# Gated delta rule: 32x32 diagonal blocks inverted on VectorE beside the gate projection, two TensorE levels left

## What is computed

```
proj = x @ w_in                      # q, k, v (3 x 1024 columns), gate z (1024), a, b
q, k, v = silu(causal_conv4(proj[qkv]))
q = l2_norm(q) * 128**-0.5;  k = l2_norm(k)
beta = sigmoid(b);  g = cumsum(-exp(A_log) * softplus(a + dt_bias))      # per chunk
decay[i, j] = exp(g[i] - g[j]) for i >= j
lower = strictly_lower((k * beta) @ k.T * decay)
u, w = solve(I + lower, [v * beta, k * beta * exp(g)])      # unit lower triangular
attn = (q @ k.T) * decay
for each chunk:                      # S is the 128 x 128 state of a head
    v_new = u - w @ S
    o = (q * exp(g)) @ S + attn @ v_new
    S = S * exp(g_last) + (k * exp(g_last - g)).T @ v_new
o = rms_norm(o) * silu(z);  mix = o @ w_out
```

## Time and profile before

| | us |
|---|---|
| three timed runs | 2270.66, 2274.2, 2274.4 (median 2274.2) |
| the profiled execution, own time | 2272.42 |
| its span in the profile | 2270.7 |
| column loop: first convolution 43.7 to last qkv matmul 175.8 | 132.1 |
| gate steps to the end of block 1 (175.8 to 252.0) | 76.2 |
| delta rule, block 2 (252.0 to 449.2) | 197.2 |
| mixer output, block 3 (449.2 to 523) | 73.8 |
| everything behind it | 1747 |

### The profile page before, as it was taken

The page is one execution under the profiler, slowest core; times in us unless marked ns, Lnnn a source line. Parts: engine busy times, 40 slices in busy tenths (PEclk is TensorE's granted clock), DMA queues, the critical chain, the costliest instruction groups (busy, mean ns, idle before and its releaser), DMA issues. The chain is left out here.

```text
span 2270.7 us, 35278 instructions
## 1 busy us (share of the span) xinstructions
PE 2089.2 (92%) x9789; PEld 1580.8 (70%) x9789; DVE 1512.7 (67%) x2511; ACT 1307.8 (58%) x2174; POOL 478.7 (21%) x367
## 2 busy tenths in 40 slices
PE   7998899899999999999995899999999999999994
PEld 6875799885677677777764655685766766777772
DVE  3762556556788778878773314746877777888884
ACT  3333244533687777877774223532777777777774
POOL 0000355400122222322221300001232222222220
PEclk9999999999999999999998799998999999999997
DMA  5321100015799999999998110026999999999994
GB/s 189 102 82 56 43 20 20 20 44 213 292 371 372 356 351 356 369 365 368 359 351 266 47 60 29 32 76 241 333 346 349 355 354 345 367 366 370 372 361 144
DMA packets 181905, 539.80 MB, mean 238 GB/s; under 512 B 26528, under 2 KB 58176, under 8 KB 181696
## 3 DMA queue, kind: packets, MB, share of 16 engines
q1 hardware_dynamic: 151776, 460.75, 54.2%
q0 software_dynamic: 25248, 69.25, 12.1%
q10 hardware_dynamic: 4800, 8.78, 1.0%
HBM read 504.71 MB, written 54.10 MB: 246 GB/s over the span
## 5 line engine op out<-in xcount | busy, mean ns | idle before, releaser
L1779 DVE TENSOR_TENSOR gu_l<-ring,gu_h 128x1024 fp32r<-128x1024 f32 x512 | 610.2, 1220 | 98.2 <-ACT gu_h L1643 82.0
L1643 ACT CAST gu_h<-ring 128x1024 fp32r<-128x1024 f32 x512 | 523.2, 1059 | 88.2 <-DMA ring<-in_moe_w_up 72.4
L1558 PE MATMUL bank<-gu_h,xgT_l 128*128 128x512 f32 x1024 | 413.5, 404 | 0.0
L1560 PE MATMUL bank<-gu_h,xgT_h 128*128 128x512 f32 x1024 | 401.3, 392 | 0.0
L1559 PE MATMUL bank<-gu_l,xgT_h 128*128 128x512 f32 x1024 | 400.4, 391 | 0.0
L1907 POOL DMA_INDIRECT xg<-h_rows,list_idx x128 | 146.9, 1147 | 904.2 <-issue 476.4
L1610 PE MATMUL bank<-ring,hmT_f 128*128 128x512 f32 x536 | 273.3, 591 | 0.0
L1650 ACT CAST down_h<-ring 128x1024 fp32r<-128x1024 f32 x128 | 134.1, 1047 | 221.2 <-DMA ring<-in_moe_w_down 131.8
L1926 POOL DMA_INDIRECT moe_sum<-y,out_idx x128 | 196.8, 1538 | 171.8 <-issue 152.6
L1785 DVE TENSOR_TENSOR down_l<-ring,down_h 128x1024 fp32r<-128x1024 f32 x128 | 156.7, 1225 | 103.9 <-ACT down_h L1650 96.6
L1560 PEld LDWEIGHTS bank<-gu_h,xgT_h 128*128 128x128 f32 x1024 | 192.9, 188 | 42.4
(11 more groups left out here) (375 smaller groups left out, 3351.8 us busy)
## 6 DMA issues: line engine op xcount, KB each, us to landing
ring<-in_moe_w_gate SPq DMA_DIRECT2D x256, 512.0 KB
ring<-in_moe_w_up SPq DMA_DIRECT2D x256, 512.0 KB
ring<-in_moe_w_down SPq DMA_DIRECT2D x256, 512.0 KB
ring<-in_a_w_in SPq DMA_DIRECT2D x32, 512.0 KB
ring<-in_a_w_out SPq DMA_DIRECT2D x8, 512.0 KB
h_rows<-ring ACTq DMA_DIRECT2D x8, 512.0 KB, 2.6
moe_sum<-y ACTq DMA_DIRECT2D x8, 512.0 KB, 6.3
ring<-moe_sum SPq DMA_DIRECT2D x8, 512.0 KB, 5.0
```

The source lines that it names most:

```text
L1558: nc.tensor.matmul(out, lhsT=xl, rhs=wh, start=k == 0, stop=False)
L1560: last = nc.tensor.matmul(out, lhsT=xh, rhs=wh, start=False, stop=k == KD - 1)
L1643: nc.scalar.copy(gu_h[:, c, :, :], gate_up_cols(gate_slot, c * CH // 2, CH // 2)).then_inc(gu_hi.sem, 1)
L1779: nc.vector.tensor_tensor(gu_l[:, c, :, :], gate_up_cols(gate_slot, c * CH // 2, CH // 2), gu_h[:, c, :, :].bitcast(F32), ALU.subtract).th ...
```

## The change

**What it does.** The decay, the products of keys and queries, and the inverse of all 128 diagonal 32x32 blocks move out of block 2 into block 1. In the column loop PE makes the sums of g behind c = 2, ACT reads them at c = 3 and stores them to DRAM, loads them back to all partitions at c = 4 (2 MB), builds the distances (32 operations of 128x128) at c = 6 to 13 and their exponentials (128x2048) at c = 9 and 13. From c = 17 on PE makes two units of key products per column and DVE multiplies them with the decay. ACT packs the diagonal blocks (strided copies), DVE transposes them so that one partition holds whole systems, and eliminates 31 columns (two operations each) between the gate steps; the inverses are transposed back at the end of block 1. The squares shrink to the 8 columns of q and stand beside gate steps 10 to 13, and ACT instead of DVE takes the gate out of PSUM, through Silu. In block 2 two levels remain (32 to 64: `product5`, `inverse5`; 64 to 128: `product6`, `inverse6`), and those of tile tt + 1 are issued among the scan of tile tt. The constants shrink from 17 planes to 7. Since the system takes ring slots 10 and 11, x is loaded a second time in block 2; w_out is loaded there too, and the router's weights have a tile of their own.

The scan of a tile and the inverse of the next one alternate. The diff, cut to its core:

```diff
+                def gate_rows():
+                    act.wait_ge(cols_ready.sem, cols_ready.base + 1)
+                    nc.scalar.activation(ecol[:, :, :, :], bank[3][:, 0:2 * TT * H].rearrange("p (a t h) -> p a t h", a=2, t=TT), ACT.Exp)
+                    nc.scalar.activation(gcol_neg[:, :, :], bank[3][:, 0:TT * H].rearrange("p (t h) -> p t h", t=TT), ACT.Copy, scale=-1.0)
+                    nc.scalar.copy(row_parts, bank[2][0:H, :].rearrange("p (t q) -> p t q", q=P))
+                    link(act, "act", nc.scalar.activation(row_parts2, bank[2][0:H, :].rearrange("p (t q) -> p t q", q=P), ACT.Exp))
+                    for kind, rows in enumerate((row_parts, row_parts2)):
+                        act.dma_start(gain_row[kind].rearrange("t h q -> h t q"), rows).then_inc(row_stored.sem, 16)
+                def load_gate_rows():
+                    act.wait_ge(row_stored.sem, row_stored.base + 32)
+                    act.dma_start(sym, gain_row[0].partition_broadcast(P)).then_inc(gate_rows_in.sem, 16)
+                def distances(first):
+                    if first == 0:
+                        act.wait_ge(gate_rows_in.sem, gate_rows_in.base + 16)
+                    tt, h0 = divmod(first, H)
+                    for h in range(h0, h0 + 4):
+                        last = nc.scalar.activation(sym[:, tt, h, :], sym[:, tt, h, :], ACT.Abs, bias=gcol_neg[:, tt, h:h + 1])
+                    if first % 16 == 12:
+                        link(act, "act", last)
+                def decays(half):
+                    nc.scalar.activation(sym[:, 2 * half:2 * half + 2, :, :], sym[:, 2 * half:2 * half + 2, :, :], ACT.Exp, scale=-1.0).then_inc(sym_done.sem, 1)
+                def pack(half):
+                    act.wait_ge(kq_done.sem, kq_done.base + 2 * KQ_PAIRS * (half + 1))
+                    for b in range(QUADS):
+                        dst = packed[quad(b), :, 2 * H * half:2 * H * (half + 1)]
+                        src = ring[quad(b), 10 + half, :].rearrange("p (m q) -> p q m", q=P)[:, quad(b), :]
+                        last = nc.scalar.copy(dst, src)
+                    last.then_inc(packed_done.sem, 1)
...
+                    if c == 3:
+                        gate_rows()
+                    elif c == 4:
+                        load_gate_rows()
+                    elif 6 <= c < 14:
+                        distances(4 * (c - 6))
+                        if c in (9, 13):
+                            decays((c - 9) // 4)
+                    elif c == N_QKV - 2:
+                        pack(0)
+                act_z_hi(act, 0)
+                act_z_hi(act, 1)
+                pack(1)
+                for n in range(2, 2 * KD):
+                    if n >= KD + 4:
+                        square_pair(n - KD - 4)
                     act_z_hi(act, n)
+                    if n == KD - 2:
+                        act.wait_ge(norms_ready.sem, norms_ready.base + 1)
+                        nc.scalar.activation(k_norm[:, :, :], k_norm[:, :, :], ACT.Sqrt).then_inc(k_root.sem, 1)
+                    elif n == KD + 1:
+                        act_open_gate(act, 0)
...
+                    if c == 2:
+                        gate_sums()
                     if c > 2 * H:
                         transpose_v(c - 1 - 2 * H)
+                        keys_queries(2 * (c - 1 - 2 * H))
+                        keys_queries(2 * (c - 1 - 2 * H) + 1)
+                for u in range(2 * H - 2, KQ_UNITS):
+                    keys_queries(u)
...
+                    if KD + 2 <= n < KD + 6:
+                        sum_squares(2 * (n - KD - 2))
+                        sum_squares(2 * (n - KD - 2) + 1)
+                    elif n == KD + 6:
                         transpose_sums()
...
+                def decayed(u):
+                    tt, pair = divmod(u, KQ_PAIRS)
+                    if u % (2 * KQ_PAIRS) == 0:
+                        v.wait_ge(sym_done.sem, sym_done.base + u // (2 * KQ_PAIRS) + 1)
+                    v.wait_ge(kq_ready.sem, kq_ready.base + u + 1)
+                    c0 = tt % 2 * H * P + pair * 2 * P
+                    dst = ring[:, 4 + tt // 2:11 + tt // 2:6, c0:c0 + 2 * P].rearrange("p a (h q) -> p a h q", q=P)
+                    src = kq_bank(u)[:, :].rearrange("p (h a q) -> p a h q", a=2, q=P)
+                    by = sym[:, tt, 2 * pair:2 * pair + 2, :].unsqueeze(1).to_broadcast([P, 2, 2, P])
+                    nc.vector.tensor_tensor(dst, src, by, ALU.mult).then_inc(kq_done.sem, 1)
...
+                def systems():
+                    v.wait_ge(packed_done.sem, packed_done.base + 2)
+                    own(nc.vector.transpose(ring[:, 9, 0:BLOCK], ring[:, 8, 0:BLOCK]))
+                    own(nc.vector.tensor_single_scalar(sq_sys[:, :], ring[:, 9, 0:BLOCK:SUB + 1], EPS, ALU.add))
+                    nc.vector.transpose(k_norm[:, :, :].rearrange("p t h -> p (t h)"), sq_sys[:, :]).then_inc(norms_ready.sem, 1)
+                    own(nc.vector.reciprocal(gain_sys[:, :], sq_sys[:, :]))
+                    own(nc.vector.tensor_tensor(gain_sys[:, :], gain_sys[:, :], beta_sys[:, :], ALU.mult))
+                    own(nc.vector.tensor_tensor(lower, lower, gain_sys[:, :].unsqueeze(2).to_broadcast([P, SUB, SUB]), ALU.mult))
+                def eliminate(j):
+                    rows, cols = SUB - 1 - j, j + 1
+                    part = outer[:, 0:rows * cols].rearrange("p (i c) -> p i c", c=cols)
+                    own(nc.vector.tensor_tensor(part, lower[:, j + 1:, j:j + 1].to_broadcast([P, rows, cols]), solved[:, j:j + 1, 0:cols].to_broadcast([P, rows, cols]), ALU.mult))
+                    own(nc.vector.tensor_tensor(solved[:, j + 1:, 0:cols], solved[:, j + 1:, 0:cols], part, ALU.subtract))
+                def inverses():
+                    by = gain_sys[:, :].unsqueeze(1).to_broadcast([P, SUB, SUB])
+                    own(nc.vector.tensor_tensor(X_sys.rearrange("p (c i) -> p i c", i=SUB), solved, by, ALU.mult))
+                    own(nc.vector.tensor_tensor(Y_sys.rearrange("p (i c) -> p i c", c=SUB), solved, by, ALU.mult))
+                    nc.vector.transpose(ring[:, 8, BLOCK:2 * BLOCK], X_sys)
+                    nc.vector.transpose(ring[:, 9, BLOCK:2 * BLOCK], Y_sys)
...
+                    if c > 2 * H:
+                        decayed(2 * (c - 1 - 2 * H))
+                        decayed(2 * (c - 1 - 2 * H) + 1)
+                dve_z_lo(v, 0)
+                for u in range(2 * H - 2, KQ_UNITS):
+                    decayed(u)
+                dve_z_lo(v, 1)
+                v.wait_ge(z_identity.sem, z_identity.base + 2)
+                systems()
+                low, spent = 2, 1.8
+                for j in range(SUB - 1):
+                    while low < KD + 6 and spent >= 1.8:
+                        dve_z_lo(v, low)
+                        low, spent = low + 1, spent - 1.8
+                    eliminate(j)
+                    spent += 0.4 + 0.00208 * (SUB - 1 - j) * (j + 1)
+                for n in range(low, KD + 6):
                     dve_z_lo(v, n)
+                copy_sums()
+                dve_z_lo(v, KD + 6)
+                dve_z_lo(v, KD + 7)
+                inverses()
+                norms()
...
+                for tt in range(-1, TT):
+                    ahead = tt + 1 < TT
+                    for g in range(2):
+                        if tt < 0:
+                            keys_T(0, g)
+                        elif tt > 0:
+                            from_state(tt, g)
+                        if ahead:
+                            product5(tt + 1, g)
+                    for g in range(2):
+                        if tt >= 0:
+                            from_values(tt, g)
+                        if ahead:
+                            inverse5(tt + 1, g)
+                    for g in range(2) if ahead else ():
+                        if tt >= 0:
+                            keys_T(tt + 1, g)
+                        transpose_X(tt + 1, g)
+                        product6(tt + 1, g)
+                    for g in range(2) if ahead else ():
+                        inverse6(tt + 1, g)
+                    for g in range(2) if ahead else ():
+                        values_keys(tt + 1, g)
...
+                def systems_x(tt):
+                    act.wait_ge(x_done.sem, x_done.base + 2 * tt)
+                    for b in range(QUADS):
+                        nc.scalar.copy(X0[quad(b), :, quad(b)], X_packed[quad(b), :, H * tt:H * tt + H].rearrange("p c h -> p h c"))
+                    for b in (0, 2):
...
+                systems_y(0)
+                act_open_gate(act, 1)
+                for tt in range(-1, TT):
+                    ahead = tt + 1 < TT
+                    if tt >= 1:
+                        root(tt - 1)
+                    for g in range(2) if ahead else ():
+                        act.wait_ge(p5_ready.sem, p5_ready.base + at(tt + 1, g))
```

(35 more changed lines are left out.)

837 lines of the change are left out of this document (309 added, 528 removed).

## The result

| | before | after |
|---|---|---|
| median of 4 runs, us | 2272.43 | 2194.94 |
| lowest, highest | 2268.09, 2274.4 | 2189.83, 2197.87 |
| profiled execution, own time | 2272.42 | 2189.83 |

The ratio of after to before is 0.9659, 95% interval 0.9647 to 0.9671: 77.5 us less. The forecast was 2182 with a range of 2158 to 2214. The changed kernel, run again later beside other kernels, gave 0.9657 (0.9638 to 0.9676).

The account below looks back on a forecast made before the run. TensorE was taken to bound block 2, and a ring as full as TensorE the column loop. −2 + 35.7 − 14.2 − 111.2 = −91.7 from 2272.4 gives 2180.7, stated as 2182 us; range 2158 to 2214.

Parts of the forecast that it names:

- full ring: Column loop: convolution, Silu, rounding and low part wait on each other, 5.51 us per column; ScalarE work behind the Silu adds.
- rival A: Column loop absorbs ScalarE's distances and exponentials in slack, so 25 us go: 2157 us; chance 12%.
- the exponentials: Column loop: two of 128x2048 at 1.95 us, each with two table loads of 1.28 and links: 4.6 each, 9.2 together.
- c = 3 and 4: Column loop: an exponential and a Silu with table loads, four small activations, three DMA issues; 5.2 us including sums of g.
- Rival D: ScalarE: a table switch costs as much again as its load, 6 × 1.28, 8 us: 2190 us; chance 5%.
- The sums of squares: Gate steps 10 to 13 carry them on TensorE, 0.86 us each; these steps take 14.3 us.
- Rival B: Gate steps: VectorE bounds them through elimination and low parts, packs and inverses at doubled price; 14 more, 2196 us; chance 18%.
- The packs: Before gate step 2: ScalarE packs four strided blocks of 32x512, 0.6 to 1.05 us each.
- the hand-overs: Block 2: copies and subtractions passing between engines from product5 to inverse6 lie beside the state's products in the scan.
- the prologue: Start of block 2, tile 0's inverse with nothing beside it: VectorE places blocks for 4.5 us; 19 us in all.
- rival C: Block 2: TensorE's clock stays at 1.2 GHz through the prologue and one scan tile, about 20 us more: 2202; chance 12%.
- Rival E: Pauses at c = 3, 4, 9 and 13 lower TensorE's clock lastingly: +96, +38 and +70, about 2390 us; chance 3%.

Follow-up runs that it names:

- the added operations: Against the changed kernel, the first of the two operations of each eliminated column is issued twice, 31 more on VectorE: ratio 0.9676 (0.9661 to 0.9690).

## Why the prediction held, and which terms were off

**Column loop, +35.7 against +33.1.** The reading as a full ring was right, and rival A (work absorbed) is refuted by the run without distances: 16.4 us came back for the work taken out. Distances cost 6.69 − 5.51 = 1.18 per column (forecast 1.2), the sums of g 1.3 (1.3), key products 1.8 per column (1.73). The term that was too large is the exponentials: 3.2 us each for two of them where 4.6 was taken, since the second load lies beside the convolution. The same held at c = 3 and 4: 3.6 and 0.4 us in place of 5.2. What the forecast had at nothing is the clock inside the loop: 1.3 us in column 14. Rival D, a switch dearer than its load, is refuted: it was cheaper, and in the rows the exponential starts 1.30 us after the load (105.27 and 106.57), so nothing is added between the load and a long activation, which the rows of before had left open.

**Gate steps, −14.2 against −10.3.** Step 2 starts 15.5 us after the last column's matmuls, as forecast. Two terms were missed. The sums of squares take 1.8 us a step, not 0.86; the forecast counted one column of squares per step where there are two. And a pause of 3.75 us ahead of step 2 lowers the clock to 0.66 for 5 us. Rival B, VectorE as the bound, is refuted by the added operations: there were about 8 us of room. The packs cost 1.1 us each, just above the upper end.

**Block 2, −111.2 against −98.6.** The work on TensorE was right: once the wait is gone an iteration takes 19.8 us (forecast 19.6 to 20.8). What failed is the sentence that the hand-overs lie beside the state's products: the copies of u and w stand ahead of them, and nothing is beside these. ScalarE's placing was priced (4 to 6 us; it is 6.6), but put ahead of u and w in the prologue alone, and there with 3 of it seen (the wait was 3.87). It stands in the same place in the iterations of tiles 0 and 1 too, and holds up the whole scan. Moving half of it gave back 12 us. The second miss is the prologue: VectorE's clearing and placing 8.8 us, not 4.5; handing X to ScalarE gave 3.7. From the block's start to the first scan 25.5 us go by where the forecast had 19.

**The clock (rival C)** was right in part, and in addition to the forecast rather than in place of it: the waits cost a second time, 1.6 us an iteration by the run with products in the waits, where the forecast had 2.5 us for all of block 2. The measured 2194.9 is near the 2196 of rival B, but by another mechanism, so that is chance. Rival E didn't come near: the column loop ran at 0.96. (Its own terms add to 204 us, so the 92 us that would decide are 45% of them, not 43.)

**The sum** was −91.7 in one execution, and −82.7 came, of which 6.5 lie in the start and behind block 3 and are within what these vary. The three stages that the change touches give −75.8 against a forecast of −89.7, and that agrees with the medians' 77.5. So the column loop as a ring, the hidden elimination and TensorE's work in block 2 were read rightly, the hand-overs of block 2 were not, and 14 us of the gain were missed: 12.6 in block 2 and 3.9 in the gate steps, less the 2.6 that the column loop was cheaper. That the −82.7 of the profile lie nearer to the forecast is luck of that execution. Of the signs named ahead of the result, columns 9 and 13 were 3.2 us longer than column 10, not 5, and a scan tile was 24.3 us, not 20, just inside the 25 that would have refuted the forecast.
